# Turning the second head of a pair at the end of the stage instead of five tiles later

## The reference, cut to what matters

```
h    = rmsnorm(x, norm_mix)
qa..vc = split(h @ w_in)
oa   = window_attention(...)        # 8 heads of 64, bias from a table, a sink
ob   = neighborhood_attention(...)  # 8 heads of 64, bias from a table
oc   = axial_global_attention(...)  # 16 heads of 64, rotary, no bias
x    = x + concat(rmsnorm(oa), rmsnorm(ob), rmsnorm(oc)) @ w_o
h    = rmsnorm(x, norm_mlp)
x    = x + relu(h @ w_up)**2 @ w_down
```

```
s = einsum('bqgrd,bkgd->bgrqk', q, k) * scale
p = softmax(s)
o = einsum('bgrqk,bkgd->bqgrd', p, v)
```

## Time and profile before

| | us |
|---|---|
| median of 3 runs | 3302.31 |
| lowest and highest | 3301.84, 3302.68 |
| the profiled execution | 3302.07 |
| its span, first to last instruction | 3300.3 |
| TensorE busy | 3266.6 (99%) |
| DVE busy | 2169.5 (66%) |
| ACT busy | 1621.1 (49%) |
| mean granted clock of TensorE | 0.997 of 2.4 GHz |

### The profile page before, as it was taken

The page is one execution under the profiler, slowest core; times in us unless marked ns, Lnnn a source line. Parts: engine busy times, 40 slices in busy tenths (PEclk is TensorE's granted clock), DMA queues, the critical chain, the costliest instruction groups (busy, mean ns, idle before and its releaser), DMA issues.

```text
span 3300.3 us, 48398 instructions
## 1 busy us (share of the span) xinstructions
PE 3266.6 (99%) x19112; PEld 2858.4 (87%) x19112; DVE 2169.5 (66%) x3068; ACT 1621.1 (49%) x2692; POOL 913.5 (28%) x815
## 2 busy tenths in 40 slices
PE   8999999999999999999999999999999999999998
PEld 7989888888888887788888888889788888888887
DVE  5668676755676668778774477555778775457654
ACT  4457464444444545555443444444655544344443
POOL 2434132210232224254320033112326321013221
PEclk9999999999999999999999999999999999999999
DMA  7544546755565554555556555555355565555564
GB/s 257 189 166 148 177 155 208 234 192 187 190 190 192 186 181 138 158 169 182 189 190 195 183 191 191 192 191 176 123 176 170 186 190 190 195 185 188 189 195 142
DMA packets 188280, 604.57 MB, mean 183 GB/s; under 512 B 36597, under 2 KB 41573, under 8 KB 188054
## 3 DMA queue, kind: packets, MB, share of 16 engines
q1 hardware_dynamic: 188054, 601.47, 56.2%
HBM read 599.16 MB, written 8.00 MB: 184 GB/s over the span
## 4 chain that ended last, share of the span: by engine, by line
PE 86%; DVE 9%; ACT 3%; issue 1%; POOL 1%; DMA 0%; SPq 0%; DVEq 0%; POOLq 0%; ACTq 0%
PE ps L1794 86%; DVE wl L2402 4%; DVE x L2410 1%; DVE xr L2402 1%; ACT sS L2236 1%; ACT wh L2140 1%; PE ps L1797 1%; DVE sS L2406 1%; DVE den L2546 0%; ACT tA L2140 0%; DMA wt<-in_w_vsl 0%; DVE qb L2410 0%; DMA wt<-in_w_in 0%; POOL den L2761 0%; POOL acc L2761 0%
## 5 line engine op out<-in xcount | busy, mean ns | idle before, releaser
L2402 DVE TENSOR_TENSOR wl<-wt,wh 128x1024 fp32r<-128x1024 f32 (+2 forms) x1104 | 1465.3, 1359 | 317.5 <-ACT wh L2140 301.1
L1794 PE MATMUL ps<-x,wh 128*128 128x512 f32 x4448 | 1563.8, 394 | 17.1 <-DVE x L2410 16.1
L2140 ACT ACTIVATE wh<-wt 128x1024 fp32r<-128x1024 f32 (+2 forms) x1104 | 1117.8, 1051 | 281.0 <-PE ps L1794 242.5
L1794 PE MATMUL ps<-x,wl 128*128 128x256 f32 x4448 | 1255.1, 282 | 0.0
L1794 PEld LDWEIGHTS ps<-x,wh 128*128 128x128 f32 x4448 | 836.7, 188 | 198.9 <-DVE wl L2402 11.7
L1794 PEld LDWEIGHTS ps<-x,wl 128*128 128x128 f32 x4448 | 842.8, 189 | 0.6
L1794 PE MATMUL ps<-ua,wh 128*128 128x512 f32 (+1 forms) x2432 | 832.0, 386 | 0.0
L1794 PE MATMUL ps<-ua,wl 128*128 128x256 f32 x2368 | 667.4, 282 | 0.0
L2402 DVE TENSOR_TENSOR tB<-ps,tA 128x256 f32<-128x256 f32 x422 | 177.0, 423 | 727.7 <-ACT tA L2140 727.5
L2140 ACT ACTIVATE tA<-ps 128x256 f32<-128x256 f32 x422 | 158.8, 380 | 948.8 <-PE ps L1794 948.5
L1794 PE MATMUL ps<-ub,wh 128*128 128x512 f32 x1536 | 536.6, 390 | 0.0
(11 more groups left out here) (233 smaller groups left out, 1854.3 us busy)
## 6 DMA issues: line engine op xcount, KB each, us to landing
wt<-in_w_up SPq DMA_DIRECT2D x384, 512.0 KB, 4.3
wt<-in_w_down SPq DMA_DIRECT2D x384, 512.0 KB, 4.8
wt<-in_w_in SPq DMA_DIRECT2D x156, 512.0 KB, 4.6
wt<-in_w_o SPq DMA_DIRECT2D x64, 512.0 KB, 4.5
wt<-in_w_out SPq DMA_DIRECT2D x32, 512.0 KB, 4.0
wt<-in_w_vb SPq DMA_DIRECT2D x16, 512.0 KB, 4.2
wt<-in_w_va SPq DMA_DIRECT2D x16, 384.0 KB, 3.7
wt<-in_w_vsl SPq DMA_DIRECT2D x8, 512.0 KB, 6.2
```

Of the source, the lines that this page charges most:

```text
L1794: return eng.matmul(o, l, r, start=start, stop=stop, skip_group_check=True)
L2140: return eng.activation(o, i, ACT.Copy, **kw)
L2402: return eng.tensor_tensor(o, a, b, op)
```

## The change

The second head's turn no longer goes into `late` but into a list of its own, `turns`, and `step_bg` runs that list after the tasks have advanced. So it stands at the end of the stage, before tile 8, and not before tile 13. `turns` is emptied in every stage.

```
-    late = []
+    late, turns = [], []
 
     def step_bg():
         held["s1"] = 0
         for g in list(tasks):
             if next(g[0], "end") == "end":
                 tasks.remove(g)
                 g[1]["done"] = True
+        run_all(turns)
         at13.extend(late)
         late.clear()
...
         turn_head(hds[0], pts[0], 0)
-        late.append(lambda: turn_head(hds[1], pts[1], 1))
+        turns.append(lambda: turn_head(hds[1], pts[1], 1))
         yield
```

## The result

| | before | after |
|---|---|---|
| median, us | 3302.49 | 3310.09 |
| lowest and highest of 12 | 3301.65, 3304.76 | 3308.75, 3311.15 |
| the profiled execution | 3302.07 | 3311.15 |
| its span | 3300.3 | 3309.3 |

The ratio is 1.0021, with a 95% interval of 1.0014 to 1.0028: 7.6 us more, +0.23%, slower. The forecast was 3310.7 us (8.4 more).

The account below looks back on a forecast made before the run. TensorE was taken to bound the kernel (busy 99%, 86% of the chain). Per layer 1.75 + 1.04 + 1.74 - 0.33 = 4.20 us, 8.4 for two, gave 3310.7 against 3302.31 us (+0.25%), range 3305 to 3316.

Parts of the forecast that it names:

- The wait at C6 and C7: Second turn waits for ACT's copy of the first head: 1.75 us at C6 plus 1.04 at C7 a layer.
- C0 to C5 cost nothing: Early C pairs stall TensorE, but it is off the chain there; later waits swallow the delay: 0 us.
- Rival 1: All stalls reach the end: C0 to C5 add 5.8 us a layer, B2 0.78; 3323.9 us, chance 0.06.
- Rival 4: Nothing visible: the copy is done when TensorE gets there, so the stall is hidden; 3302.3 us, chance 0.04.
- B2 and B3: B3's wait swallows B2's delay of 0.78; together 1.74 us a layer, 2.52 as the other end.
- Rival 2: Behind B3, ACT and DVE carry the stretch, so only C6 and C7 count: 4.9 us, 3307.2, chance 0.17.
- The restarts: At A1, A2, B0 and B1 one TensorE restart fewer gains 0.08 us each, 0.33 a layer.
- The sum: Attention of each layer: 1.75 + 1.04 + 1.74 - 0.33 = 4.20 us, 8.4 for two layers.
- rival 3: TensorE's clock falls at C6 and B3 in both layers: 8.4 + 9.7 = 18.1 us, 3320.4, chance 0.06.
- The price of a fall: One fall of TensorE's clock costs 2.4 us, half of the 4.85 us busy at the lower level.

Follow-up runs that it names:

- `bank_after`: Changed kernel (turn before tile 8) with second heads of C6, C7 and B3 turned into their own bank `bM`: 3302.21 against 3302.35 us, ratio 1.0000.
- `place_11`: Against the kernel before, all second heads turned before tile 11, three tiles behind the stage: 3304.19 us, ratio 1.0005.
- `bank_before_2`: Kernel before (turn before tile 13) with bank `bM` for second heads of C6, C7 and B3, timed again: 3301.26 against 3302.46 us, ratio 0.9995.

## Why the prediction was right, step by step

**The wait at C6 and C7, right to a tenth.** Worked out 1.75 + 1.04 = 2.79 a layer; the shifts are 2.79 and 2.79, in the second trace of after 2.80 and 2.79. The cover's length is confirmed by the place before tile 11 and the cause by the second bank.

**C0 to C5 cost nothing, right** (0.01 us in the trace of after, no shift when moved alone). Rival 1, all stalls reach the end, falls with it. Its price took C1's stall of 1.04 us for all six pairs; C0's is longer, with 1.92 us of idle TensorE, and was swallowed too. Rival 4, nothing visible, falls with the 7.6 us. One consequence I had not drawn: their delay makes TensorE late at C6, so the wait there is shorter (1.59 us, and 2.08 with C6 and C7 moved alone), while the cost, set by the copy's time, is the same.

**B2 and B3, the size was off.** Forecast 1.74 at B3, and it was there at its product (1.71 to 1.73 in five of the six layers traced, for the sixth see the sum), but DVE's stretch behind it gave 0.63 to 0.70 back: in the five, 1.03 to 1.08 stayed. The prediction let all of it pass through DVE's stretch, and that is the step that was too simple; the last term of the sum should have been 1.05. Why this stretch takes back some of it was not tried. ACT's `tA` of 1479.37 moved to 1485.49 in after, 6.12 later, of which 5.49 was left at the next `rT`. At B3 about 2 us of idle TensorE were forecast. 1.18 stand in the second trace of after, since TensorE comes there later from B2, and 0.79 in the first, where it is late from the norm as well; again the copy's time sets the cost, not the length of the wait. Rival 2, part of it is absorbed, is thus somewhat more than a third true, and its place was named rightly.

**The restarts, wrong.** -0.33 a layer was counted for A and B pairs whose two turns now stand together. Measured is 0, at each of the four pairs, when they are moved alone. The rows of after at A1 show it: two turns in a row and the next tile:

```profile
1389.34 1.09 PE L1798 MATMUL ps<-idt,sS 128*128 128x128 f32 x8
1390.19 0.47 PE L1795 MATMUL ps<-x,wh 128*128 128x512 f32 x1
```

From turn to tile are 0.85 us for both. Apart, in before, they took 0.41 (1385.62 to 1386.03) and 0.36 (1387.86 to 1388.22): 0.77. The restart saved, 0.08, is paid in the turns. The 0.08 that I took off at C6 and C7 was there by the sum, so this term is only wrong where no stall stands between the turns.

**What was not foreseen: 0.5 us at the norm of C**, first layer, in the profiled execution of after. Timeline:

```profile
1449.77 0.71 PE L1795 MATMUL ps<-idt,den 128*128 128x128 f32 x4 [1.11 <-POOL den L2762]
```

Its chain goes back over POOL to a load of the bias:

```profile
1438.58 4.29 DMA sS<-rpm
...
1442.94 1.24 POOL sS L2762 x2
...
1448.07 1.66 POOL den L2762
...
1449.77 9.71 PE ps L1795 x58
```

The second trace of after has no such wait in that place, one of the traces with C6 and C7 alone has it (0.92). So it isn't bound to the moved turns of the later pairs. I take it for a matter of the single execution; what makes it come was not tried.

**The sum.** Forecast a layer 2.79 + 1.74 - 0.33 = 4.20. Measured by the pairs it is 2.79 + 1.05 + 0 = 3.84, so 7.7 for two layers, and the medians say 7.6. The forecast increase of 8.4 is 0.7 above that: B3 was 0.69 a layer too high, and the restarts, 0.33 a layer the other way, cancel half of it. That cancelling is luck; the two C terms, which carry 5.6 of it, are not.

The single trace of after has 4.55 and 3.97, since more is in it than the change. In its first layer 0.48 comes at the norm of C, and B2 and B3 add 1.29 and not 1.05, because ACT's copy at B3 is 4.41 later than before (1464.11 to 1468.52) where its neighbours are 4.20: 2.79 + 0.48 + 1.29 = 4.56. In the second the jump at about 2443 us adds 0.16: 2.79 + 0.16 + 1.03 = 3.98. Less the 0.51 at the last transposition that leaves 8.0 for this execution. The second trace of after has 4.03 and 3.79.

**The clock, rival 3, came true in part and cost nothing in after.** Windows of after at C0 of the first layer (wait, behind it) and at C6 (wait, behind it):

```profile
1285.40:1287.40 2.00, 0.09 (x1) 0.02 (x1) 1.54 (x2) 1.86 (x3) 0.99 (x2) 0.84 0.00 0
1287.40:1290.80 3.40, 3.39 (x14) 3.02 (x15) 3.22 (x10) 0.00 (x0) 0.00 (x0) 0.59 0.50 190
...
1342.00:1344.90 2.90, 1.33 (x12) 0.65 (x9) 2.17 (x2) 2.78 (x5) 0.90 (x1) 1.00 0.00 0
1344.90:1350.00 5.10, 5.08 (x31) 4.58 (x32) 3.25 (x11) 1.63 (x3) 1.50 (x2) 1.00 0.64 206
```

Before, the two first stretches have a clock of 1.00. In after it fell at C0 within 1.92 us of idle, where TensorE has slack and the slower tiles are swallowed, and not at C6, where they would have counted. At C0 of the first layer it fell in all four traces in which C0's turn stands before tile 8 (after twice, C0 to C5 alone, `bank_after`), each with 1.92 us of idle, and at C0 of the second layer, with 1.29 to 1.33 us, in none of them. In `place_11`, with 0.77 us, it did not fall either.

My reason against this rival was that 2 us are short beside the 3.74 that had cost the clock. It was wrong, and the trace of before could have told it. Windows of before: the 3.74 us of idle, which began at 492.41, in two parts:

```profile
492.40:494.00 1.60, 0.01 (x1) 0.00 (x0) 1.60 (x3) 0.96 (x3) 1.60 (x1) 1.00 0.13 51
494.00:496.10 2.10, 0.00 (x0) 0.00 (x0) 2.10 (x3) 1.06 (x3) 1.81 (x3) 0.50 0.66 191
```

The clock was down 1.6 us after the idle stretch had begun. And it fell not once but twice in before: from about 3289.5 us to the end it is 0.50 again, behind an idle stretch of 1.93 us and within one of 1.04. The price of a fall was sized at 2.4 us and measured as 1.57.

The Trainium skill ("TensorE: Matmul & The Clock Gate", Part 4, on PE-mode transpose) says transposes do not count as busy for the clock. The falls at C0 and C6 agree in part: a turn stands right behind the idle time at both, and right ahead of it at C6 (at C0 scores stand between). But the two of before come with no transposition in the ten us (484 to 494) and the six us (3283 to 3289) ahead of them. No run here puts other matmuls in their place, so that the transpositions are the reason is not shown.

**Left open:** why the clock falls in some of a set of like stretches and not in others, why DVE's stretch takes back some of B3's delay, and the jumps at the norm of C and at about 1403 and 2443 us.

## What to carry to other kernels

Before an instruction is moved forward, look at what it waits for: tiles that stand ahead of it are cover, and moving it past n tiles costs up to n tiles' time, less the slack, where its engine is on the chain (here 2.79 us a layer at two pairs), and nothing where a later wait swallows it. Work out when the resource comes back (end of the copy + 0.14 us) and put the waiting instruction there, but also ask when its own consumer, here a copy in DVE's order, must have it. If two heads share one bank, a second bank is worth more than any order: here it took the whole loss away with the turn still in the early place.

## What the hardware showed unexpectedly

- TensorE's granted clock fell to 0.50 within or right behind idle stretches of 1.92 us (C0 of the first layer, four traces of four) and 2.08 to 2.10 us (C6, two of six stretches of 2.07 to 2.11 us). It cost 1.57 us where TensorE set the end. It did not fall after 1.58 to 1.73 us at C6 (four stretches) or 1.29 to 1.33 at C0 of the second layer (four).
- Eight transpositions in a row take TensorE 0.85 us to the next tile, two groups of four 0.41 and 0.36.
- Executions are shifted by -0.2 to 2.3 us against each other before the attention begins, where the programs are the same; in after 0.8 of its 0.93 came up at 500 to 600 us of the span. Read from the ends alone, it would have been blamed on the change. The 2.3 (`bank_before_2`) came up at 500 us, where the clock was at 0.50 for 10.2 us (495.7 to 505.9) and in before for 6.8.
